# A causal attention stage on one TensorE: four score banks and one value bank in PSUM, and every engine's order drawn one score unit further ahead

## What is computed

```python
# group A, 4 heads, each with two halves c of 64 columns
s = einsum('bqhcd,bkhcd->bchqk', q, k) * 64 ** -0.5
p = masked_softmax(s, k_pos <= q_pos)                 # causal
w = p[:, 0] - lam * p[:, 1]                           # difference of the halves
oa = einsum('bhqk,bkhv->bqhv', w, v)
# group B, 4 heads of 128 columns; for a prompt of 512 the selected blocks and the
# window both come to causal attention, each with its own key and value
p = masked_softmax(q @ k.T * 128 ** -0.5, k_pos <= q_pos)
o_sel, o_win = p @ v_sel, p @ v_win
```

## Time and profile before

| | us |
|---|---|
| runs (three) | 1909.7 median, 1905.71 to 1914.84 |
| profiled execution, span | 1913.1 |
| the stage pa_, first transpose on PE to the last finish on DVE | 1004.2 to 1166.0 |
| barrier and first product of the next stage | 1169.4 |
| PE busy in all | 1684.6 (88%) |
| DVE busy in all | 808.4 (42%) |

### The profile page before, as it was taken

The page is one execution under the profiler, slowest core; times in us unless marked ns, Lnnn a source line. Parts: engine busy times, 40 slices in busy tenths (PEclk is TensorE's granted clock), DMA queues, the critical chain, the costliest instruction groups (busy, mean ns, idle before and its releaser), DMA issues. The chain is left out here.

```text
span 1913.1 us, 39025 instructions
## 1 busy us (share of the span) xinstructions
PE 1684.6 (88%) x14897; PEld 1300.9 (68%) x14897; DVE 808.4 (42%) x1592; ACT 586.3 (31%) x1353; POOL 103.8 (5%) x166
## 2 busy tenths in 40 slices
PE   6999998998998899999978887888888888369998
PEld 5888888776777677777556756666666666157776
DVE  4221222352266432334425654466455565374221
ACT  4321112231223121221115213455445455262110
POOL 3000000151000000000001000000000000020000
PEclk9999999998999999999897878999999999779999
DMA  6465555684422314124146515999999999193343
GB/s 210 154 200 184 173 188 159 220 292 127 157 70 91 110 51 127 56 83 119 47 140 238 171 41 183 358 358 384 372 384 373 374 364 378 53 332 88 122 158 115
DMA packets 218112, 373.28 MB, mean 195 GB/s; under 512 B 41917, under 2 KB 122254, under 8 KB 216614
## 3 DMA queue, kind: packets, MB, share of 16 engines
q1 hardware_dynamic: 214390, 359.24, 55.0%
q0 software_dynamic: 3248, 9.44, 1.5%
q10 hardware_dynamic: 288, 2.10, 0.3%
HBM read 334.27 MB, written 40.69 MB: 196 GB/s over the span
## 5 line engine op out<-in xcount | busy, mean ns | idle before, releaser
L370 PE MATMUL pj_ps<-pj_whi,pj_xhi 128*128 128x512 f32 (+1 forms) x1024 | 417.9, 408 | 5.9 <-PEq L86 5.9
L371 PE MATMUL pj_ps<-pj_wlo,pj_xhi 128*128 128x512 f32 (+1 forms) x1024 | 402.7, 393 | 0.0
L372 PE MATMUL pj_ps<-pj_whi,pj_xlo 128*128 128x512 f32 (+1 forms) x1024 | 401.4, 392 | 0.0
L288 DVE TENSOR_TENSOR pj_wlo<-pj_w,pj_whi 128x1024 fp32r<-128x1024 f32 (+1 forms) x128 | 156.2, 1221 | 461.1 <-ACT pj_whi L246 459.8
L246 ACT ACTIVATE pj_whi<-pj_w 128x1024 fp32r<-128x1024 f32 (+1 forms) x128 | 132.4, 1034 | 522.9 <-DMA pj_w<-in_w_in 521.5
L370 PEld LDWEIGHTS pj_ps<-pj_whi,pj_xhi 128*128 128x128 f32 x1024 | 198.3, 194 | 67.6 <-issue 30.9
L372 PEld LDWEIGHTS pj_ps<-pj_whi,pj_xlo 128*128 128x128 f32 x1024 | 198.0, 193 | 40.8
L371 PEld LDWEIGHTS pj_ps<-pj_wlo,pj_xhi 128*128 128x128 f32 x1024 | 198.8, 194 | 34.3
L1589 ACT ACTIVATE da_kT<-da_tp 128x512 f32<-128x512 f32 x200 | 119.2, 596 | 168.4 <-PE da_tp L1470 155.7
L1676 DVE COPY da_kT<-da_tp 128x512 f32<-128x512 f32 x128 | 88.5, 691 | 73.2 <-PE da_tp L1470 72.8
L3116 PE MATMUL ou_ps<-ou_whi,ou_mhi 128*128 128x512 f32 x256 | 104.7, 409 | 6.5 <-DVE ou_wlo L3040 6.5
(11 more groups left out here) (531 smaller groups left out, 2284.8 us busy)
## 6 DMA issues: line engine op xcount, KB each, us to landing
at_early_a<-in_cache_a_kv SPq DMA_DIRECT2D x128, 512.0 KB, 6.4
da_pa<-in_cache_a_kv SPq DMA_DIRECT2D x128, 512.0 KB, 6.7
pj_w<-in_w_in SPq DMA_DIRECT2D x120, 512.0 KB, 4.6
px_pages<-in_cache_b_kv SPq DMA_DIRECT2D x256, 128.0 KB, 2.5
at_early_b<-in_cache_b_kv SPq DMA_DIRECT2D x128, 128.0 KB, 6.5
da_pb<-in_cache_b_kv SPq DMA_DIRECT2D x128, 128.0 KB, 6.8
ou_w<-in_w_out SPq DMA_DIRECT2D x32, 512.0 KB, 4.3
proj<-pj_out SPq DMA_DIRECT2D x52, 256.0 KB, 5.6
```

Of the source, the lines that this page charges most:

```text
L288: dve.tensor_tensor(self.wlo[:, r, :, 0:n], self.w[:, r, :, 0:n], self.whi[:, r, :, 0:n], ALU.subtract).then_inc(self.wlo_ready, 1)
L370: pe.matmul(acc, hi, high, start=kc == 0, stop=False)
L371: pe.matmul(acc, hi, low, start=False, stop=False)
L372: last = pe.matmul(acc, lo, high, start=False, stop=kc == KC - 1)
```

## The change

Two constants, BANKS = 4 and AHEAD = 2, take the place of a 3 and a 1 that were written into the code. The scores get a fourth bank, and po keeps one bank of its two. All three engines take their units up to u(i)+2 instead of u(i)+1 in step i. `attend` of section c now waits at its first product for `finish` of section c-1, since both use the one bank.

```diff
+    BANKS, AHEAD = 4, 2
-        scores = [s.ps(f"scores{i}", [P, 512]) for i in range(3)]
+        scores = [s.ps(f"scores{i}", [P, 512]) for i in range(BANKS)]
         tp = s.ps("tp", [P, 4, P])
-        po = [s.ps(f"po{i}", [P, 4, HEAD]) for i in range(2)]
+        po = s.ps("po", [P, 4, HEAD])
...
-                    if pair[-1] >= 3:
-                        pe.wait_ge(exped, pair[-1] - 2)
+                    if pair[-1] >= BANKS:
+                        pe.wait_ge(exped, pair[-1] - BANKS + 1)
...
                     c = 3 * t + sec
-                    if h == 0 and c >= 2:
-                        pe.wait_ge(finished, c - 1)
+                    if h == 0 and c >= 1:
+                        pe.wait_ge(finished, c)
...
                     if i < NV:
-                        while done <= min(pvs[i][0] + 1, NU - 1):
+                        while done <= min(pvs[i][0] + AHEAD, NU - 1):
                             done += score(done)
```

More of the change, by code:

```diff
@@ L1164, in score @@
                         kn = P // len(pair)
-                        pe.matmul(scores[x % 3][:, 0:n], k.attT[p0:p0 + kn, qc, P * t:P * t + P],
+                        pe.matmul(scores[x % BANKS][:, 0:n], k.attT[p0:p0 + kn, qc, P * t:P * t + P],
                                   k.attT[p0:p0 + kn, kc, 0:n], start=True, stop=False)
                     for x in pair:
-                        pe.matmul(scores[x % 3][:, n - P:n], one[:], late[:], start=False, stop=True).then_inc(scored, 1)
+                        pe.matmul(scores[x % BANKS][:, n - P:n], one[:], late[:], start=False, stop=True).then_inc(scored, 1)
                     return len(pair)
@@ L1187, in attend @@
                     c = 3 * t + sec
-                    if h == 0 and c >= 2:
-                        pe.wait_ge(finished, c - 1)
+                    if h == 0 and c >= 1:
+                        pe.wait_ge(finished, c)
                     pe.wait_ge(copied, i + 1)
                     for b in range(t + 1):
-                        last = pe.matmul(po[c % 2][:, h, :], wT[:, i % 2, b, :],
+                        last = pe.matmul(po[:, h, :], wT[:, i % 2, b, :],
                                          k.rows_p[:, b, vcol:vcol + HEAD], start=(b == 0), stop=(b == t))
@@ L1224, in exp @@
                         act.wait_ge(weighted, sum(1 for v in pvs if v[2] == 0 and v[0] <= u - 5))
-                    act.activation(e[:, u % 6, 0:n], scores[u % 3][:, 0:n], ACT.Exp, bias=nm[:, u:u + 1],
+                    act.activation(e[:, u % 6, 0:n], scores[u % BANKS][:, 0:n], ACT.Exp, bias=nm[:, u:u + 1],
                                    accum_out=l[:, u:u + 1]).then_inc(exped, 1)
@@ L1255, in row_max @@
                     dve.wait_ge(scored, u + 1)
-                    dve.tensor_reduce(nm[:, u:u + 1], scores[u % 3][:, 0:n], AX_X, ALU.max,
+                    dve.tensor_reduce(nm[:, u:u + 1], scores[u % BANKS][:, 0:n], AX_X, ALU.max,
                                       negate=True).then_inc(maxed, 1)
@@ L1292, in finish @@
                     if sec == 0:
-                        dve.tensor_copy(out, po[c % 2][:]).then_inc(finished, 1)
+                        dve.tensor_copy(out, po[:]).then_inc(finished, 1)
                         return
@@ L1297, in finish @@
                     dve.wait_ge(divisors, 2 * t + sec)
-                    dve.tensor_tensor(out, po[c % 2][:], r[:, u - 3:u + 1].unsqueeze(2).broadcast_to(
+                    dve.tensor_tensor(out, po[:], r[:, u - 3:u + 1].unsqueeze(2).broadcast_to(
                         [P, 4, HEAD]), ALU.mult).then_inc(finished, 1)
```

## The result

The changed kernel took 1921.6 us in the median of seven runs (1916.8 to 1929.7), the one before 1909.7 us (seven runs, 1903.1 to 1914.8). The ratio is 1.0081, with a 95% interval of 1.0059 to 1.0103: 15.5 us slower, between 11.3 and 19.7. The medians lie 11.9 us apart. The profiled execution's span is 1919.1 us against 1913.1.

A forecast was written before the change was run, and what follows sets the result against it. PE's order of work, with gaps, bounds one 162 us stage between barriers. Edges 15.55 us less gains 4.8 gives +10.75, plus 1 for the clock: +12 us, median 1921.7 us, range 1907 to 1932.

The forecast's parts named there:

- the sum of edges and gains: Stage pa_: section edges cost 15.55 us, removed score waits give back 4.8 us, net +10.75 us before the clock.
- +1 for the clock: Stage pa_: new gaps of 3 us and more lower PE's clock; +1 us taken from between 0 and +8.
- The waits that the fourth bank removes: `score` waiting for an exponential, ten waits: 9.4 us falls to under 1.5, net gain 4.8 us.
- the ring of DVE's list: Tile 3, steps 36 to 38: DVE's own list sets the pace, L966 to `turn` some 4.15 us instead of 5.03.
- The new wait: PE's L1193 at section edges waits for DVE's `finish`: ten entries, about 5 us in step 38, 15 to 20 us in all.
- Sections 4 and 5: Section 5's edge costs 1.5 us; section 4's is swallowed by PE's wait for DVE's guest, with 1.4 us more.
- Section 3: Edge where DVE does two maxima, `weigh`, `copy`, `finish`: product 3 us late, part given back, 2.2 us lost.
- Tile 2: Step 25: both maxima ahead of `weigh`, where guest L798 waits too; one short wait goes; +0.3 us net.
- Sections 10 and 11: Edges where PE's product waits for `finish`: 2.65 us at section 10, 1.4 us at 11, partly overlapped by the end chain.
- Section 9: Worst edge: DVE's whole step starts only after PE's guest; 2.3 to 4.4 us lost, 3.4 taken, low clock believed.
- The clock rival: Stage pa_: clock falls with each new gap, +19 to +24 us, 1929 to 1934; sign: clock under 0.75; chance 0.20.
- my own case: Whole kernel: the forecast of +12 us within 4 either way; chance 0.42.

The follow-up runs named there:

- the second execution: The kernel before profiled once more with no edit: stage 158.3 us at a clock of 0.83, where the first was 161.8 at 0.81.
- the long edge alone: Kernel before, both value banks kept, product waits for `finish` of the section just before only at sections 3, 9 and 10: stage 174.8 us, ratio 1.0100.
- the short edges with both banks: Kernel before, both value banks kept, that wait only at sections 1, 2, 4, 5, 6, 7, 8 and 11: stage 168.5 us, ratio 1.0071.

## Why the prediction was right

The direction and the mechanism were right; the size came out a quarter low. The agreement of 1921.7 with the measured median of 1921.6 is luck in part: by the ratio the loss is 15.5 us (11.3 to 19.7), not 12, and the stage's is 16.2 against one execution of the kernel before and 19.7 against the other. The forecast's sum of waits was good and its price of the clock was not: PE idled 12.1 us more (11.6 against the second execution), where the sum of edges and gains was 10.75, and was busy 4.1 us more (8.1) with the same instructions, where I had put +1 for the clock. Below, the offsets are without the unit scored ahead.

- **The waits that the fourth bank removes.** Forecast: 9.4 us to under 1.5. Measured: none left. Tile 0 gave back 1.2 us against 1.0. Two of the ten waits lay in tile 1 (0.65 and 0.62 us, steps 13 and 14), for which the prediction has no term; in their place `turn` waited 0.84 and 0.53 us for DVE's copies. In tile 3 the offset fell by 4.2 us from step 35 to step 38, forecast were 3.0; the ring of DVE's list was as read: from L966 at 1124.57 to `turn` at 1128.76 are 4.19 us, forecast 4.15. From step 39 to step 42 it fell by 1.5 us, forecast was 0.3. This last is chance in the execution of before that it is compared with. Its steps 39 to 42 ran at a clock of 0.69, those of the second execution at 0.88, and the changed kernel took 13.65 us for them at 0.87:

```profile
1133.33:1149.36 16.03, 14.20 (x62) 10.52 (x61) 7.76 (x14) 3.00 (x8) 0.54 (x1) 0.69 0.09 33
```

```profile
1125.60:1139.80 14.20, 11.20 (x63) 8.22 (x61) 7.76 (x14) 3.01 (x8) 0.54 (x1) 0.88 0.10 38
```

- **The new wait.** Forecast: ten entries, one of about 5 us in step 38, 15 to 20 us in all. Measured: ten, 4.96 in step 38, 19.4 in all. Section 6 was free, as read from the earlier trace rows. Section 7 waited 1.38 us and section 11 1.59; forecast costs 1.5 and 1.4. Moving `finish` took all but 0.7 us of it away, and the wait alone, with two banks, brought all of it.
- **Sections 4 and 5.** Together with the guest's wait they were forecast at +0.1 us, and the offset went from +4.6 to +4.5. The second execution of before was 1.5 us faster here, so the agreement is no closer than that.
- **Section 3, a term that was mis-sized.** I took 2.2 us. The offset rose by 3.4 between steps 12 and 16, and the long edge alone, with both banks, cost 4.1. PE waited 2.42 us there, and DVE's step, 3.0 us from one `copy` to the end of `finish`, was no longer than forecast (3.36); but behind the gap the clock fell and the products ran at half speed, which I had left to a lump sum.
- **Tile 2, the second.** I took +0.3 us net for steps 23 to 26, and the offset rose by 3.9 (4.0 against the second execution). 1.6 us of it are in the guest's L798, 32 products of eight columns, which took 4.18 us before:

```profile
1071.00 5.75 PE L798 MATMUL pa_cy<-pa_kcT,ap_attT 128*128 128x8 f32 x32 [0.24 <-DVE pa_kcT L914]
```

```profile
1061.00:1068.00 7.00, 6.61 (x29) 4.86 (x30) 1.86 (x5) 0.72 (x3) 0.00 (x0) 0.50 0.52 168
```

Behind the wait of section 5 the clock was 0.50 for 7 us, where PE was busy nearly all the time and nothing covered it. That this wait brought the clock down is not shown. It had fallen ahead of it, behind a wait of 2.20 us for DVE's copy: two masks (L1169) that take 0.44 us at the full clock took 0.69, and the product that waited came after them.

```profile
1058.93 0.69 PE L1169 MATMUL pa_scores<-pa_late,pa_one 128*128 128x128 f32 x2
...
1061.39 1.22 PE L1193 MATMUL pa_po<-ap_rows_p,pa_wT 128*128 128x128 f32 x4 [1.33 <-DVE pa_o L1299]
```

And in the kernel with the long edges alone, whose section 5 waits for nothing, L798 ran at the low clock too:

```profile
1049.29 1.06 PE L1192 MATMUL pa_po<-ap_rows_p,pa_wT 128*128 128x128 f32 x4
...
1058.50 6.24 PE L798 MATMUL pa_cy<-pa_kcT,ap_attT 128*128 128x8 f32 x32 [0.23 <-DVE pa_kcT L914]
```

Its steps 23 to 26 took 15.7 us, as did those of before with early `finish` (L798 6.26 us), against 13.6 in before and 17.5 in the changed kernel; with one value bank and one unit ahead L798 took 3.74 us, although that kernel has the wait. So where the low clock falls in tile 2 changes from one execution to the next, and how much of the 3.9 us the change caused stays open.
- **Sections 10 and 11, the third.** I took 2.65 + 1.4 = 4.05 us, and the offset rose by 7.1 from step 42 to the end. With the gap filled it was 2.8 us less, so 4.3 us: the waits were priced well, and the low clock behind section 10 was missing. In before and its second execution this stretch took 16.6 us both times, so this difference is hardly chance.
- **Section 9.** Forecast 3.4 us between 2.3 and 4.4 (the 7.75 us in it should be 7.85 with its own terms). From the guest's end at 1130.47 to `turn` at 1140.87 are 10.4 us; less the 4.6 of before and 1.75 for the unit ahead it is 4.1, and with both banks and nothing scored ahead 4.4: the upper end, at the low clock as I had believed. The offset rose by only 2.7, because L846 and `turn` on either side ran at the low clock before and not after.
- **The clock rival** (slower still). By its own sign, a clock under 0.75, it did not hold: the stage's was 0.80, hardly under before's 0.81 and 0.83. But the 16.2 us lie at the upper end of my own case (+12 within 4), and what was missing is what this rival named. Its price was too high: the short edges with both banks ran at 0.85, so that the gaps of 1.5 us do not all lower the clock.
- **The Trainium skill's** remark on a second PSUM buffer without further gain ("TensorE: Matmul & The Clock Gate", "HAM oscillation — how this bites in real kernels") does not hold for this order, in which one value bank is 1.03% slower and two with the wait of one 1.46%, and does hold once `finish` stands earlier: then one bank (1.0004) and two (1.0013) are equal within the intervals. What made the difference in these runs is what stands between the last product and the evacuation in the other engine's list.

## What to carry to other kernels

What a second buffer was worth here depended on where the instruction that frees the first one stands in the other engine's list. Before paying for a second bank, or giving one up, look at that place: behind a guest piece that itself waits for PE, PE waited 5.0 us (section 9), and with `finish` one step earlier 0.3 us at most. And sum a stall with what it does to the clock behind it, if PE is the engine without slack there: the waits here were forecast to within 1.4 us (12.1 of idling against 10.75), the clock's part was not.

## What the runs showed of the hardware

- The granted clock differs between executions of the same kernel at the same place: the stage of the kernel before ran at 0.81 and at 0.83, 161.8 and 158.3 us, with nearly the same waits; its steps 39 to 42 ran at 0.69 and 0.88, 16.0 and 14.1 us. A difference of under 4 us in one stage can't be read from one profile of each kernel.
- The low clock doubled the time of the wide products and not that of the narrow ones. Eight products of 128 columns (L1193) took 2.08 and 1.06 us. The 32 products of eight columns (L798) took 6.24 us at the low clock and 3.74 us at the full one (with one value bank and one unit ahead), 1.67 times as long; a single one was recorded with 361 and 256 ns.
- Whether a gap of 2.6 us was idle or filled with work decided the clock behind it at section 10: 2.08 us idle against 1.16 filled for the same product. It need not fall at once. With two banks and the wait, the product behind the same idle gap still ran at the full clock and the scores behind it did not:

```profile
1162.69 1.16 PE L1192 MATMUL pa_po<-ap_rows_p,pa_wT 128*128 128x128 f32 x8 [2.58 <-DVE pa_o L1293]
1163.69 1.84 PE L1165 MATMUL pa_scores<-ap_attT 128*128 128x512 f32 x2
```
